# Odd layer's attention logits: one full-precision product replaced by three products of high and low parts

## The reference

```python
q = rms_norm(q.reshape(bsz, L, C_HEADS, C_HEAD_DIM), q_g)
k = rms_norm(k.reshape(bsz, L, C_KV_HEADS, C_HEAD_DIM), k_g)
...
_, idx = lax.top_k(score, topk)
valid = idx <= t[None, :, None]
...
logits = jnp.einsum('bqhgd,bqkhd->bqhgk', q_blk, k_sel).astype(jnp.float32) * (Dh ** -0.5)
...
logits = jnp.where(valid[:, :, None, None, :], logits + bias, NEG_INF)
p = jax.nn.softmax(logits, axis=-1).astype(v.dtype)
return jnp.einsum('bqhgk,bqkhd->bqhgd', p, v_sel)
```

## Time and profile before

| what | value |
|---|---|
| median of 3 runs | 2011.0 us (2010.79 to 2011.02) |
| the profiled execution's own time | 2010.99 us |
| its span, first to last instruction | 2009.7 us |
| mean granted TensorE clock | 0.993 of full speed |
| busy: PE, DVE, ACT, POOL | 1944.4, 1438.2, 882.5, 620.8 us |
| attention stage, from the last gate projection to the output projection | about 811 to 985 us |

### The profile page before, as it was taken

How to read it: one execution, slowest core, us unless ns; L and a number is a source line. 1 busy time by engine, 2 the same in 40 slices (tenths; PEclk the granted TensorE clock), 3 DMA queues, 4 the chain that set the end, 5 groups by cost and what they waited for, 6 DMA issues and landing times.

```text
span 2009.7 us, 24201 instructions
## 1 busy us (share of the span) xinstructions
PE 1944.4 (97%) x9108; PEld 1504.4 (75%) x9108; DVE 1438.2 (72%) x2198; ACT 882.5 (44%) x1573; POOL 620.8 (31%) x428
## 2 busy tenths in 40 slices
PE   8999989999999999999999999999999999999997
PEld 6777867787548787666787887888777877777785
DVE  7668686522379997455357799899997887685639
ACT  5343285333457751545212333544226764352431
POOL 3554410552101122545352000000003673235443
PEclk9999999999999999999999999999999999999999
DMA  6322330442501122311333211111142223455322
GB/s 271 128 72 83 114 123 22 167 158 69 151 22 33 53 76 82 105 42 53 123 98 105 74 54 63 53 53 53 57 147 86 79 74 145 163 191 195 112 85 105
DMA packets 72428, 197.90 MB, mean 98 GB/s; under 512 B 11182, under 2 KB 20559, under 8 KB 71800
## 3 DMA queue, kind: packets, MB, share of 16 engines
q1 hardware_dynamic: 72168, 196.35, 28.9%
q10 hardware_dynamic: 144, 0.00, 0.0%
HBM read 152.89 MB, written 46.71 MB: 99 GB/s over the span
## 4 chain that ended last, share of the span: by engine, by line
PE 47%; DVE 30%; ACT 4%; issue 3%; DMA 2%; POOL 1%; SPq 0%; DVEq 0%; ACTq 0%
PE psum L266 44%; DVE m L2973 10%; DVE m L2187 4%; PE psum L269 3%; DVE m L2994 2%; DVE m L321 2%; DMA m<-in_w 1%; POOL m L311 1%; ACT m L301 1%; DVE m L540 1%; DVE m L456 1%; DVE m L531 1%; DVE m L3172 1%; DVE m L3111 1%; DVE m L3175 1%
## 5 line engine op out<-in xcount | busy, mean ns | idle before, releaser
L266 PE MATMUL psum<-m,m 128*128 128x512 f32 (+10 forms) x8308 | 1862.1, 393 | 40.1 <-DVE m L321 9.8
L266 PEld LDWEIGHTS psum<-m,m 128*128 128x128 f32 (+4 forms) x8308 | 1418.6, 186 | 454.0 <-issue 137.7
L311 POOL TENSOR_TENSOR m<-m,m 128x1024 fp32r<-128x1024 f32 (+1 forms) x122 | 307.9, 2527 | 1002.3 <-ACT m L301 1002.2
L301 ACT ACTIVATE m<-m 128x1024 fp32r<-128x1024 f32 (+2 forms) x166 | 173.4, 1048 | 342.1 <-PE psum L266 208.5
L2973 DVE SCALAR_TENSOR_TENSOR m<-m,m,m 128x1024 f32<-128x1024 f32 x240 | 312.3, 1303 | 6.3
L269 PE MATMUL psum<-m,m 128*128 128x128 f32 x784 | 110.6, 277 | 12.1 <-ACT m L1450 6.1
L269 PEld LDWEIGHTS psum<-m,m 128*128 128x128 f32 x784 | 89.6, 141 | 33.3 <-ACT m L1450 8.0
L2187 DVE TENSOR_SCALAR_CACHE_REDUCE m<-m,m 128x896 bf16<-128x896 f32 (+4 forms) x130 | 102.8, 847 | 1.1
L2519 POOL TENSOR_TENSOR m<-m,m 128x384 f32<-128x384 f32 (+5 forms) x48 | 72.5, 1528 | 55.9 <-DVE m L2311 37.2
L2407 ACT ACTIVATE m<-m,m 128x1024 bf16<-128x1024 f32 (+1 forms) x62 | 64.1, 1035 | 26.4 <-DVE m L2214 26.4
L2311 DVE CUSTOM_DVE_ANT_0 m<-psum,m 128x128 f32<-128x128 f32 (+3 forms) x64 | 48.3, 755 | 37.9 <-PE psum L266 36.7
(11 more groups left out here) (314 smaller groups left out, 1652.9 us busy)
## 6 DMA issues: line engine op xcount, KB each, us to landing
m<-in_w SPq DMA_DIRECT2D x164, 512.0 KB, 3.7
scr_hscr<-m SPq DMA_DIRECT2D x4, 2048.0 KB, 6.6
m<-scr_hscr SPq DMA_DIRECT2D x4, 2048.0 KB, 10.6
scr_turned<-scr_strip SPq DMA_DIRECT2D x8, 575.5 KB, 12.6
m<-in_x SPq DMA_DIRECT2D x4, 1024.0 KB, 7.9
scr_gscr<-m SPq DMA_DIRECT2D x16, 256.0 KB, 4.2
m<-in_x SPq DMA_DIRECT2D x2, 2048.0 KB, 8.8
m<-scr_turned SPq DMA_DIRECT2D x8, 512.0 KB, 4.5
```

The source lines that it names most:

```text
L266: return self.nc.tensor.matmul(out, lhsT, rhs, start=start, stop=stop, skip_group_check=True)
L301: k.nc.scalar.activation(k.hi[SLOT[i]][:, 0:kk * n], k.raw[i % 2][:, 0:kk * n], ACT.Copy).then_inc(*k.up("w_hi", i))
L311: k.nc.gpsimd.tensor_tensor(lo, raw, hi.bitcast(F32), ALU.subtract).then_inc(*k.up("w_lo", i))
```

## The change

The logits become three products of float32r parts. Queries and keys are split as the weight panels are: the high part of a head is a copy by ScalarE (`query_high`, `key_high`), the low part a subtraction by GpSimd in halves of 512 (`query_low`, `key_low`), written in place over the head. Heads of the queries are split while the head before is in work: `query_high(n+1)` stands behind unit (n, 2) on ScalarE, `query_low(n+1)` behind the `s0` of units (n, 5) and (n, 6) on GpSimd. Key head 0 and query head 0 are split in the gate's projection, key head 1 at units (1, 4) on ScalarE and (2, 5), (2, 6) on GpSimd. The high parts have buffers of their own, two for queries and two for keys.

```diff
@@ -1896,6 +1896,9 @@
         self.pts = [k.tile(X0, [4, 4, 128]), k.tile(X0 + 8 * KB, [8, 4, 128])]
         self.gts = [k.tile(X0 + (24 + 4 * i) * KB, [1024]) for i in range(2)]
         self.MH, self.ML = k.tile(PH, [8, 1024], F32R), k.tile(X0 + 32 * KB, [8, 1024], F32R)
+        self.QL, self.KL = k.tile(PH, [8, 1024], F32R), k.tile(PH + 32 * KB, [2, 1024], F32R)
+        self.qh = [k.tile(O + 4 * KB, [1024], F32R), k.tile(H0 + 16 * KB, [1024], F32R)]
+        self.kh = [k.tile(O, [1024], F32R), k.tile(X0 + 60 * KB, [1024], F32R)]
         self.smr = [k.tiny[:, 128 + 8 * i:136 + 8 * i] for i in range(3)]
 
         self.sums, self.recs = ([k.tiny[:, o + 4 * i:o + 4 * i + 4] for i in range(2)] for o in (152, 160))
@@ -2070,12 +2073,15 @@
             pe.wait_ge(*at("od_L", *two))
         else:
             pe.wait_ge(*at("head", O.norms[-1], 1))
-        pe.wait_ge(*at("head", n, b // 4))
+        kv, bs = n // 4, slice(128 * b, 128 * b + 128)
+        pe.wait_ge(*at("od_qh", n))
+        pe.wait_ge(*at("od_kh", kv))
+        pe.wait_ge(*at("od_ql", n, b // 4))
         for half in range(b // 4 + 1):
-            pe.wait_ge(*at("head", 8 + n // 4, half))
+            pe.wait_ge(*at("od_kl", kv, half))
         bank = O.pairs[b % 2]
         for c, e in O.chunks(b):
-            ins = k.mm(k.bank(bank + c // 512)[:, 0:e - c], O.QT[:, n, 128 * b:128 * b + 128], O.KT[:, n // 4, c:e], True, True)
+            ins = k.mm3(k.bank(bank + c // 512)[:, 0:e - c], (O.qh[n % 2][:, bs], O.QL[:, n, bs]), (O.kh[kv][:, c:e], O.KL[:, kv, c:e]), True, True)
         ins.then_inc(*up("od_S", n, b))
 
     def s2(n, b):
@@ -2419,6 +2425,24 @@
             act.wait_ge(*at("score", 2))
         A.activation(O.row(n)[:, 512 * half:512 * half + 512], bank, ACT.Copy).then_inc(
             *up("head_raw", n, half, also=[("free", "od_proj", *use)]))
+
+    def key_high(kv):
+
+        for half in range(2):
+            act.wait_ge(*at("head", 8 + kv, half))
+        if kv:
+            act.wait_ge(*at("og_ps", 7, 1))
+        A.activation(O.kh[kv], O.KT[:, kv, :], ACT.Copy).then_inc(*up("od_kh", kv))
+
+    def query_high(n):
+
+        for half in range(2):
+            act.wait_ge(*at("head", n, half))
+        if n == 1:
+            act.wait_ge(*at("og_out", 7))
+        if n >= 2:
+            act.wait_ge(*at("od_S", n - 2, 7))
+        A.activation(O.qh[n % 2], O.QT[:, n, :], ACT.Copy).then_inc(*up("od_qh", n))
 
     def key_value(what, *key):
         if what == "ok":
@@ -2463,6 +2487,11 @@
             A.activation(O.gev[m % 2][:, 512 * half:512 * half + 512], k.bank(O.proj[("og", m, half)]), ACT.Silu).then_inc(
                 *up("og", m, half, also=[("free", "od_proj", "og", m, half)]))
         act_panel(k, PANEL_AT[f"og{m}"] + 4)
+        if m == 3:
+            key_high(0)
+        if m == 5:
+            act.wait_ge(*at("keep", 5))
+            query_high(0)
 
     def s1(n, b):
         nk, i = 128 * (b + 1), 8 * n + b
@@ -2492,6 +2521,10 @@
             s2(*O.units[i - 2])
         if i >= 4 and O.units[i - 4][1] % 4 == 3:
             s3(O.units[i - 4][0], O.units[i - 4][1] // 4)
+        if i < len(O.units) and O.units[i][1] == 2 and O.units[i][0] < 7:
+            query_high(O.units[i][0] + 1)
+        if i < len(O.units) and O.units[i] == (1, 4):
+            key_high(1)
     k.mark("od_att")
     scalar_out(k, "oo", k.H, "ln0", lambda: act_transposes(k, k.second.x0, "xs", None, (0,)), lambda: k.marks(act, "od_att"))
     k.mark("odd")
@@ -2506,8 +2539,23 @@
     pool.wait_ge(*last("causal"))
     G.affine_select(out=O.TN, in_=O.TN, compare_op=ALU.is_ge, fill=-3e38, base=0, pattern=[[-1, 128]], channel_multiplier=1).then_inc(*up("causal"))
     panels = ["qi0", "qi1", "qi2", "qi3", "ki", "ok0", "ok1", "ov0", "ov1", *(f"oq{m}" for m in range(8)), *(f"og{m}" for m in range(8))]
+    def key_low(kv, half):
+        o = slice(512 * half, 512 * half + 512)
+        pool.wait_ge(*at("od_kh", kv))
+        G.tensor_tensor(O.KL[:, kv, o], O.KT[:, kv, o], O.kh[kv][:, o].bitcast(F32), ALU.subtract).then_inc(*up("od_kl", kv, half))
+
+    def query_low(n, half):
+        o = slice(512 * half, 512 * half + 512)
+        pool.wait_ge(*at("od_qh", n))
+        G.tensor_tensor(O.QL[:, n, o], O.QT[:, n, o], O.qh[n % 2][:, o].bitcast(F32), ALU.subtract).then_inc(*up("od_ql", n, half))
+
     for name in panels[:-1]:
         pool_panel(k, PANEL_AT[name] + 4)
+        if name in ("og4", "og5"):
+            key_low(0, int(name == "og5"))
+        if name == "og6":
+            query_low(0, 0)
+            query_low(0, 1)
 
     def s0(n, b):
         if b >= 2:
@@ -2531,6 +2579,12 @@
             s0(*O.units[i + 1])
         if i >= 7 and O.units[i - 7][1] % 4 == 3:
             s3(O.units[i - 7][0], O.units[i - 7][1] // 4)
+        if i + 1 < len(O.units) and O.units[i + 1][1] in (5, 6):
+            n, half = O.units[i + 1][0], O.units[i + 1][1] - 5
+            if n < 7:
+                query_low(n + 1, half)
+            if n == 2:
+                key_low(1, half)
     k.mark("od_att")
     pool_out(k, "oo", "ln0", lambda: k.marks(pool, "od_att"))
     k.mark("odd")
```

## The result

The changed kernel takes 2007.77 us (median of 15 runs, 2005.72 to 2010.77) against 2011.56 for the kernel before beside it (15 runs, 2009.60 to 2015.03). The ratio is 0.9981, with a 95% interval of 0.9973 to 0.9989: 3.8 us less, between 2.2 and 5.4. The prediction was 2.0 less. The profiled execution took 2005.85 us, 5.1 less than that of before.

What follows compares the result with a forecast made beforehand. The prediction took TensorE's own instruction list to bound the attention stage. It summed -3.6 (stage), +0.4 (gate's store) and +1.2 (gate's projection) to -2.0 us on 2011.0, giving 2009.0 us, range 2005.0 to 2013.0.

Steps and rivals of the forecast that it cites:

- products alone, a head: Logits in the attention stage: three single-pass products shorten TensorE's list by 1.26 us a head, 10.0 us in all.
- an ordinary head (20.6): Attention stage: a head takes 20.6 us instead of 21.44, as waits give back some 0.4 of 1.26.
- head 0: First head of the attention stage: both subtractions fall into GpSimd's run without a pause, making it 1.5 us longer.
- head 2: Attention stage: one half of key head 1 more on GpSimd, 1.28 us, makes this head 0.4 us longer.
- head 7 and entry: End and start of the attention stage: head 7 splits nothing, and it and the entry save 1.15 us.
- attention stage: All heads and the entry together: 3.6 us less.
- store of the gate: ScalarE's copy of head 1's high part waits for the gate's last store: +0.4 us, bounds 0 and 1.
- gate's projection: Key head 0's low part on GpSimd holds up VectorE, delaying TensorE's norms: +1.2 us, bounds 0 and 1.3.
- the first rival: Logits: the narrow pass of 128 columns costs 0.22 us, giving 2011.2 us; chance 0.30.
- The rival of exposed weight loads: Logits pieces of 128 and 256 columns: each pass waits for its own weight load, +8 us, 2019; chance 0.06.
- The second rival: Attention stage: TensorE's waits don't come, the list alone counts, 2002.2 us, or 2006 for half; chance 0.14.
- the fourth rival: ScalarE gets late: gate's store lands after 818, or its copy delays block 3's exponential each head, 2013 us; chance 0.07.

Runs made afterwards that it cites:

- low_behind_7: Changed kernel with GpSimd making both halves of each low part behind block 7's bias and mask; 2007.32 us, 0.9971 of the kernel before.
- products_only: Changed kernel without the splits, normalised queries and keys used as they are for both parts; 2006.34 us, 0.9965 of the kernel before.
- again: The changed kernel itself, unchanged, run again as a yardstick; median 2009.63 us, 0.9984 of the kernel before.
- both_moved: Changed kernel with query low parts behind block 7 and key head 0's low part behind the last but one gate panel; 2005.59 us, 0.9964 of the kernel before.

## Why the prediction was right, and where it was off

The measured 2007.77 lies in the range, and both theory and place were right. The size was not: the forecast of 2.0 less lies just outside the measured interval of 2.2 to 5.4, and a range of 8 us would have held most outcomes, no change among them. By its own steps, against the two profiled executions:

| step | predicted | measured |
|---|---|---|
| products alone, a head | -1.26 | -1.20 |
| an ordinary head (20.6) | -0.87 | -0.95 |
| head 0 | +1.5 | +0.53 |
| head 2 | +0.4 | +0.26 |
| head 7 and entry | -1.15 | -1.1 |
| attention stage | -3.6 | -5.1 |
| store of the gate | +0.4 | 0 |
| gate's projection | +1.2 | +0.96 |
| sum | -2.0 | -4.1 |

Nearly all the misses lie on one side, towards a faster kernel, so they did not cancel.

*The passes.* The narrow one was taken at 0.11 and takes 0.29 / 3 = 0.10; the first rival (0.22) falls. The wide ones cost 0.69 for three, taken 0.68. By the gap of 216 ns in the Trainium skill (TensorE: Matmul & The Clock Gate, section on the back-to-back issue gap) it would have been 0.65, an estimate from the page's figure. The rows differ from it and decide: 0.23 a pass. The rival of exposed weight loads falls with the same rows.

*The waits.* The second rival, in which they don't come, falls for the changed kernel; with GpSimd's order changed it holds. In an ordinary head the period came within 0.1 us, but in part because two errors met: the list is worth 0.06 less than I took, and the waits take back 0.25 where I had 0.4. They are 0.2 us at block 6's seven transposes, as I had it, and 0.25 at block 7's eight (891.30 to 892.43 in the chain, 1.13 for 0.88), where I had 0.5. What failed is the size of head 0. I let TensorE wait 3.1 us there, 1.5 of it for one bank of the ring, 0.7 for the next. In the trace its idle rows are 0.79 us and 0.50:

```profile
826.56 0.66 PE L269 MATMUL psum<-m,m 128*128 128x128 f32 x4 [0.79 <-DVE m L2340]
...
827.72 0.55 PE L269 MATMUL psum<-m,m 128*128 128x128 f32 x3 [0.50 <-ACT m L2509]
```

VectorE took block 7 up at 824.67, with the stage begun half a microsecond later than before: where I had said 824.3. So GpSimd's lateness was about right, and what TensorE makes of it was too large. The rows show how much lateness is free:

| VectorE's block 7 | later than with the products alone | TensorE's loss by the period |
|---|---|---|
| head 1 (6.21 behind block 4, alone 4.98) | 1.23 | 0.25 |
| head 2 (7.43 behind block 4, alone 4.98) | 2.45 | 1.46 |
| head 0 (13.13 behind block 0, alone 10.66) | 2.47 | 1.73 |
| head 0 in the prediction (824.3 against 821.55) | 2.75 | 1.5 + 1.26 = 2.76 |

About 1 us of it reaches nobody in heads 1 and 2, and 0.7 in head 0; the prediction's price for head 0 passes all of it on. Which instant of its lists made it so can't be read from what it shows. The five ordinary heads, 0.08 better each, add 0.4.

*The gate's store* was not waited for: ScalarE's copy of head 1 begins at 815.66, right behind its operation of 815.50, so the store issued at 811.78 had landed within 3.9 us, where I had taken 5.2. The other half of the fourth rival, a copy that delays the exponential in each head, falls as well: `low_behind_7` makes the copies and its heads 1 to 6 take what they take in `products_only`, which makes none. *The gate's projection* is the exclusion that the prediction cites from the Trainium skill (SBUF — State Buffer, Who interferes with whom), and this trace agrees: L2269 stood still, 1.59 us instead of 0.63, and so did the subtraction, 2.13 us instead of 1.28 behind the waiting L2267, where the prediction had left its length at 1.28.

The sum by these rows is 4.1; the remaining 1 us between the two executions lies outside both stages (0.5 before that wait in the gate's projection, 0.5 after the stage) and is within what two executions of one kernel differ by: the 15 runs of before spread over 5.4 us. The median's 3.8 agrees with 4.1.

## What to carry to other kernels

When the bounding engine's list gets shorter, ask what else was just in time for the old list: here a split that cost an ordinary head nothing at 21.44 us a head cost 0.25 at 20.24. Put added work of a helper engine behind its last urgent item of the period, or ahead of that item only where idle time stands before it, and not merely into an engine that is idle half the time. By the rows, moving it brought 3.1 us in the stage and 0.9 in the gate's projection, nearly as much as the 4.1 that the change had brought, although the entry of that run was 1.4 us longer by its clock. And look for the instances that have no slack or more work, here heads 0 and 2: they had 3.2 of the 4.5 us lost.

## What was unexpected of the hardware

TensorE's granted clock at the stage's entry fell to half in one profiled execution of the changed kernel and not in another, after the same wait of 1.87 us (rows above), and it made the entry 1.03 us longer. Of the seven profiles with three-pass logits, that of 2761 us aside, it fell there in three (`again`, `low_behind_7`, `both_moved`); why in these is open. In each profile there are five to nine such drops of a few microseconds, some at the same place in several profiles (near 294 us in eight of the nine), others not. They go with the spread between executions of one kernel: of the 16 executions of the kernel before beside the last group, the fastest took 2009.95 us at a mean granted clock of 0.995 and the slowest 2020.01 at 0.989, with the others nearly in order between. No run sets the clock by itself, so that this is the cause is argued, not shown. Either way a gain of 4 us has to be read from the stages' rows as much as from the totals.
